# Building the one-hot products of a PEER layer in batches of eight tokens, with the weight products on GpSimd

## The reference

```python
s1 = einsum('thd,hkd->thk', q[:, :, 0], sub_keys[:, 0])   # 8 heads, 128 keys
s2 = einsum('thd,hkd->thk', q[:, :, 1], sub_keys[:, 1])
v1, i1 = top_k(s1, 16);  v2, i2 = top_k(s2, 16)
sc, ci = top_k(all sums v1 + v2, 16)
e = i1[ci // 16] * 128 + i2[ci % 16]                       # 8 * 16 = 128 experts per token
g = softmax(sc)
out[t] = sum over the 128 (e, g) of token t:  gelu(x_t . u_tab[e]) * g * v_tab[e]
```

## Time and profile before

| | |
|---|---|
| device time, three runs | 1741.38, 1743.40, 1743.91 us (median 1743.4) |
| span of the profiled execution | 1738.7 us |
| between span and the three runs | 2.7 to 5.2 us |
| stage that builds G, first to last DVE instruction | 536.9 to 657.8 us |
| DVE busy over the span | 1554.8 us (89%) |
| POOL busy over the span | 654.3 us (38%) |

### The profile page before, as it was taken

How to read it: one execution, slowest core, us unless ns; L and a number is a source line. 1 busy time by engine, 2 the same in 40 slices (tenths; PEclk the granted TensorE clock), 3 DMA queues, 4 the chain that set the end, 5 groups by cost and what they waited for, 6 DMA issues and landing times.

```text
span 1738.7 us, 29907 instructions
## 1 busy us (share of the span) xinstructions
PE 1666.5 (96%) x9344; PEld 1402.2 (81%) x9344; DVE 1554.8 (89%) x3196; ACT 866.7 (50%) x2431; POOL 654.3 (38%) x644
## 2 busy tenths in 40 slices
PE   6999999999966999999999999999999999999997
PEld 4566777866645788899989999999999988999996
DVE  3887863499999999999999999999999999999998
ACT  3222564346778995444444444444444444444443
POOL 0000000034557994444444444344444444443442
PEclk9999999999977999999999999999999999999999
DMA  9343202211135779999999999999999999999996
GB/s 357 125 141 123 74 1 78 71 61 49 61 121 173 223 201 346 396 389 401 408 395 401 405 407 401 403 409 395 396 407 399 396 406 400 402 402 403 400 400 211
DMA packets 129316, 505.91 MB, mean 291 GB/s; under 512 B 9184, under 2 KB 64096, under 8 KB 79968
## 3 DMA queue, kind: packets, MB, share of 16 engines
q0 software_dynamic: 36864, 268.45, 38.3%
q1 hardware_dynamic: 92096, 236.49, 36.5%
q10 hardware_dynamic: 288, 0.13, 0.0%
HBM read 477.18 MB, written 25.10 MB: 289 GB/s over the span
## 4 chain that ended last, share of the span: by engine, by line
DVE 35%; DMA 23%; PE 19%; issue 19%; ACT 2%; POOL 2%; DVEq 1%; SPq 0%; POOLq 0%; ACTq 0%
DMA slab<-table,ixr 22%; DVE slab L1745 9%; PE psum L501 7%; DVE slab L1695 5%; DVE ulo L1636 4%; PE psum L736 3%; DVE slab L1735 3%; DVE slab L1699 2%; DVE vlo L1722 2%; DVE slab L1730 2%; PE psum L502 2%; PE psum L666 1%; DVE wlo L1718 1%; POOL slab L1876 1%; DVE slab L1550 1%
## 5 line engine op out<-in xcount | busy, mean ns | idle before, releaser
L1876 POOL DMA_INDIRECT slab<-table,ixr x256 | 421.5, 1647 | 603.8 <-DVE slab L1745 552.2
L848 PE MATMUL psum<-hhi,uhi 128*128 128x384 f32 x1008 | 338.8, 336 | 2.4 <-issue 2.1
L848 PE MATMUL psum<-hhi,ulo 128*128 128x384 f32 x1008 | 338.2, 335 | 0.0
L848 PE MATMUL psum<-hlo,uhi 128*128 128x384 f32 x1008 | 337.6, 335 | 0.0
L1745 DVE SCALAR_TENSOR_TENSOR slab<-slab,cf 128x1024 f32<-128x1024 f32 x252 | 323.3, 1283 | 14.8 <-DVE slab L1745 0.5
L1735 DVE SCALAR_TENSOR_TENSOR slab<-slab,h2tok 128x1024 f32<-128x1024 f32 x256 | 312.2, 1220 | 26.5 <-DMA slab<-table,ixr 26.2
L862 PE MATMUL psum<-vhi,whi 128*128 128x512 f32 x762 | 297.1, 390 | 3.1 <-DVE wlo L1718 3.1
L862 PE MATMUL psum<-vhi,wlo 128*128 128x512 f32 x762 | 299.7, 393 | 0.0
L862 PE MATMUL psum<-vlo,whi 128*128 128x512 f32 x762 | 299.2, 393 | 0.0
L501 PE MATMUL psum<-slab 128*128 128x512 f32 x464 | 239.1, 597 | 2.1 <-ACT slab L929 1.7
L1210 ACT CAST whi<-slab 128x384 fp32r<-128x384 f32 x127 | 65.3, 514 | 306.7 <-DVE slab L1730 306.7
(11 more groups left out here) (237 smaller groups left out, 2801.3 us busy)
## 6 DMA issues: line engine op xcount, KB each, us to landing
slab<-ublk SPq DMA_DIRECT2D x64, 1024.0 KB
slab<-vtab SPq DMA_DIRECT2D x63, 1024.0 KB
slab<-wblk SPq DMA_DIRECT2D x90, 512.0 KB, 4.6
g_dram<-slab SPq DMA_DIRECT2D x11, 1984.0 KB, 9.0
slab<-g_dram SPq DMA_DIRECT2D x31, 704.0 KB, 8.9
slab<-table,ixr POOLq DMA_INDIRECT x256, 9.2
slab<-slab SPq DMA_DIRECT2D x42, 64.0 KB, 10.1
x<-x_in SPq DMA_DIRECT2D x1, 2560.0 KB, 9.6
```

What stands on the lines that cost most here:

```text
L848: last = pe.matmul(psum[:, b, 0:ND], w[:, c, :], m[:, c, :], start=(m_ == 0), stop=(m_ == 3 * DC - 1))
L1876: pool.indirect_dma_start(out=rows[:, sl % GR, :], out_offset=None, in_=table, in_offset=bass.IndirectOffsetOnAxis(ap=ixr[:, half, half_co ...
```

## The change

G is built in 48 batches of 8 tokens instead of 96 steps of 4. For each batch:

- DVE compares a constant `iota8` (bf16, each key number eight times) with `e2b` (bf16, the second halves) in one `tensor_tensor` of 1024 elements per partition, and writes the bf16 result to `same` (two buffers).
- DVE makes all eight `hot_a` rows in one float32 `tensor_tensor` of 1024 elements.
- POOL multiplies `same` with `gT` in one `tensor_tensor` of 1024 elements, which writes all eight `hot_b` rows (two buffers of eight rows). In batches 2 and 3 (`FETCH_IN`) DVE makes four of the rows and POOL four, and POOL issues two row fetches after each.
- ACT makes no rows. It copies PSUM out as before, in steps of 4 tokens, and no longer prepares the negated weights.
- PE issues the same matmuls in the same order; it waits for the makers at every second step.

`iota8` is filled once by a DVE `tensor_copy` before the search.

```diff
-FETCH_AT = (2, 3, 4, 5)
+BATCH = 8
+NB = ND // BATCH
+FETCH_IN = (2, 3)
...
+        iota8 = sb("iota8", [P, KEYS, BATCH], BF16)
+        e2b = sb("e2b", [P, ND], BF16)
+        e1T, gT = (sb(n, [P, ND]) for n in ("e1T", "gT"))
...
+        def by_vector(n):
+            return BATCH // 2 if n in FETCH_IN else 0
...
             for b in range(ND // 4):
+                at, half = divmod(b, 2)
+                if not half:
+                    pe.wait_ge(hot_a_set, at + 1)
+                    pe.wait_ge(hot_b_set, at + 1)
+                    if at in FETCH_IN:
+                        pe.wait_ge(hot_d_set, FETCH_IN.index(at) + 1)
                 if b >= 4:
                     pe.wait_ge(g_laid, b - 3)
                 for m in range(4):
+                    last = pe.matmul(psum[:, 4 + b % 4, m * P:(m + 1) * P], hot_a[:, at % 2, 4 * half + m, :], hot_b[:, at % 2, 4 * half + m, :], start=True, stop=True)
...
-            def distance(b):
-            def hot_row(b):
...
+            step(v.tensor_copy(iota8[:], con[:, C_IOTA:C_IOTA + KEYS].unsqueeze(2).broadcast_to([P, KEYS, BATCH])))
             v.tensor_copy(count, con[:, C_AT:C_AT + CAND].unsqueeze(2).broadcast_to([P, CAND, EARLY])).then_inc(topk_step, 1)
...
+            def hot_batch(n):
+                col, b = first_token(n), n % 2
+                if n >= 2:
+                    v.wait_ge(hot_b_set, n - 1)
+                if n - 2 in FETCH_IN:
+                    v.wait_ge(hot_d_set, FETCH_IN.index(n - 2) + 1)
+                v.tensor_tensor(same[b], iota8[:], e2b[:, col:col + BATCH].unsqueeze(1).broadcast_to([P, KEYS, BATCH]), ALU.is_equal).then_inc(same_set, 1)
+                if n >= 2:
+                    v.wait_ge(g_made, 2 * n - 2)
+                wide = [P, BATCH, KEYS]
+                v.tensor_tensor(hot_a[:, b], con[:, C_IOTA:C_IOTA + KEYS].unsqueeze(1).broadcast_to(wide),
+                                e1T[:, col:col + BATCH].unsqueeze(2).broadcast_to(wide), ALU.is_equal).then_inc(hot_a_set, 1)
+                m = by_vector(n)
+                if m:
+                    v.wait_ge(same_set, n + 1)
+                    v.tensor_tensor(hot_b[:, b, 0:m].rearrange("p t k -> p k t"), same[b][:, :, 0:m],
+                                    gT[:, col:col + m].unsqueeze(1).broadcast_to([P, KEYS, m]), ALU.mult).then_inc(hot_d_set, 1)
...
+            for n in range(NB):
+                col, b, m = first_token(n), n % 2, by_vector(n)
+                if n % (P // BATCH) == 0:
+                    pool.wait_ge(slot_set, n * BATCH // P + 1)
+                if n >= 2:
+                    pool.wait_ge(g_made, 2 * n - 2)
+                pool.wait_ge(same_set, n + 1)
+                pool.tensor_tensor(hot_b[:, b, m:BATCH].rearrange("p t k -> p k t"), same[b][:, :, m:BATCH],
+                                   gT[:, col + m:col + BATCH].unsqueeze(1).broadcast_to([P, KEYS, BATCH - m]), ALU.mult).then_inc(hot_b_set, 1)
+                if n == FETCH_IN[0]:
+                    pool.wait_ge(row_numbers_set, 1)
+                    pool.tensor_copy(ixr[:, 0, :], idxf[:, 0:8]).then_inc(ix_copied, 1)
+                    pool.wait_ge(ix_copied, 1)
+                if n in FETCH_IN:
+                    for sl in (2 * FETCH_IN.index(n), 2 * FETCH_IN.index(n) + 1):
+                        fetch_row(sl, 0, sl)
```

More of the change, by code:

```diff
@@ L263, in build @@
         e1u, e2u = (view(n, P).bitcast(U32) for n in (0, P))
-        gnT, away = view(38016, ND), view(256, 4, KEYS)
+        same = [view(c0, KEYS * BATCH // 2).bitcast(BF16).rearrange("p (k t) -> p k t", t=BATCH) for c0 in (256, 37248)]
         v_raw0 = view(35584, D)
-        hot_a, hot_b = view(9216, 4, 4, P), view(3072, 4, 4, P)
+        hot_a, hot_b = view(9216, 2, BATCH, P), view(3072, 2, BATCH, P)
         gbuf = view(19456, 2, KEYS, TG)
@@ L820, in _ @@
             for b in range(ND // 4):
-                pe.wait_ge(hot_a_set, sum(hot_a_split(n) > 0 for n in range(b + 1)))
-                pe.wait_ge(hot_b_set, b + 1)
-                pe.wait_ge(hot_c_set, b + 1)
+                at, half = divmod(b, 2)
[4 more added lines that the diff above has]
+                        pe.wait_ge(hot_d_set, FETCH_IN.index(at) + 1)
                 if b >= 4:
                     pe.wait_ge(g_laid, b - 3)
+                elif b + 4 in SLOT_BANK:
+                    pe.wait_ge(slot_set, SLOT_BANK.index(b + 4) + 1)
                 for m in range(4):
-                    last = pe.matmul(psum[:, 4 + b % 4, m * P:(m + 1) * P], hot_a[:, b % 4, m, :], hot_b[:, b % 4, m, :], start=True, stop=True)
+                    last = pe.matmul(psum[:, 4 + b % 4, m * P:(m + 1) * P], hot_a[:, at % 2, 4 * half + m, :], hot_b[:, at % 2, 4 * half + m, :], start=True, stop=True)
                 last.then_inc(g_made, 1)
@@ L1667, in number_halves @@
                 step(v.tensor_copy(e1T[:, part], e1u[:]))
-                step(v.tensor_copy(e2T[:, part], e2u[:]))
+                step(v.tensor_copy(e2b[:, part], e2u[:]))
             def halves_ready():
@@ L1688, in _ @@
             for k in range(N_DENSE):
                 v.wait_ge(slot_set, k + 1)
-                for b in range(k * P // 4, (k + 1) * P // 4):
-                    if b >= 4:
-                        v.wait_ge(g_made, b - 3)
-                    for m in range(3):
-                        col = token_of(b) + m
-                        v.tensor_scalar(hot_b[:, b % 4, m, :], con[:, C_IOTA:C_IOTA + KEYS], e2T[:, col:col + 1], gT[:, col:col + 1],
-                                        ALU.is_equal, ALU.mult)
-                    m0 = hot_a_split(b)
-                    col, wide = token_of(b) + m0, [P, 4 - m0, KEYS]
-                    v.tensor_tensor(hot_a[:, b % 4, m0:4, :], con[:, C_IOTA:C_IOTA + KEYS].unsqueeze(1).broadcast_to(wide),
-                                    e1T[:, col:col + 4 - m0].unsqueeze(2).broadcast_to(wide), ALU.is_equal).then_inc(hot_b_set, 1)
-                    within = b % (P // 4)
+                for n in range(k * P // BATCH, (k + 1) * P // BATCH):
+                    hot_batch(n)
+                    within = n % (P // BATCH)
@@ L1702, in _ @@
                     if k + 1 < N_DENSE:
[L1703 removed]
+                        if within == 9:
                             split_number(k + 1)
[L1705 removed]
+                        elif within == 10:
                             number_halves(k + 1)
[L1707 removed]
+                        elif within == 11:
                             halves_ready()
[L1709 removed]
+                    if n == 0:
@@ L1710, in _ @@
                         late_sums()
-                    elif k == 0 and within == 1:
                         row_numbers()
```

53 lines of the change are left out of this document (4 added, 49 removed).

## The result

The changed kernel takes 1801.34 us (median of 4 runs, 1797.90 to 1803.44), the kernel before 1742.39 us (median of 4). The ratio is 1.0339, with a 95% interval from 1.0322 to 1.0356: 59 us slower. The profiled execution of the changed kernel took 1802.85 us with a span of 1801.0 us.

What follows compares the result with a forecast made beforehand. DVE was taken to bound the kernel, with only the stage building G affected: 51.6 us more there, plus 0.6 and 0.5, lose 52.7 us; 1743.4 + 52.7 = 1796.1 us, range 1772 to 1822 us for 8 in 10.

Steps and rivals of the forecast that it cites:

- Exclusion of VectorE and GpSimd: Stage building G: while one engine streams two tensors, the other's waits, both ways; handover 0.01 to 0.05 us; forecast chance 0.77.
- The rival without sharing: Stage building G: path not shared in this way; 2.1 then 2.35 us a batch, 1734.9 us in all; chance 0.07.
- the one in which the bf16 comparison is exempt: Stage building G: only float32 instructions exclude POOL; period 2.95 us, 1770 us in all; chance 0.11, including sharing in parts.
- The period: Per batch of the stage: streaming 0.55 + 1.05 + 1.77 = 3.37 us, handovers and starts about 0.13 us, together 3.5 us.
- the bound from two float32 inputs: POOL's product: upper bound of 2.2 us streaming, from 2.12 ns an element; 1813 to 1818 us; chance 0.2 within the forecast.
- The estimate from the Trainium skill, GPSIMD Engine Reference, section 3.1: POOL's product: 2.25 us for 1024 elements, from 4497 ns for 2048; by it period 3.9 us, time 1815 us.
- The stage: Building G: 48 x 3.5 + 3 (other DVE work) + 1.5 = 172.5 us, 51.6 more than 120.9.
- The fetches in batches 2 and 3: POOL's row fetches, in pairs behind half a product: 8.8 us against 7.0 in the period; taken as +1.5 us.
- The 0.6 us for `iota8` and 0.5 us for the end: Filling iota8 on the chain, +0.6 us; PE's two steps left behind the last product, +0.5 us.
- The rival, over 5 us lost by the clock: Stage building G: TensorE's clock falls to its lower level, costing over 5 us on top; chance 0.05.
- `hot_a` stays at 1.20 us while products run beside it: Profile of the stage after the change: a sign that would show the prediction wrong.
- The main loop unchanged within 1 us: Profile after the change: main loop expected to stay within 1 us, as the change adds and removes nothing there.

Runs made afterwards that it cites:

- the layout run: hot_b laid out key by key, so GpSimd's product reads and writes contiguously and TensorE reads with a stride, against the changed kernel: 1813.11 us.
- the one with mixed engines: Against the changed kernel, per batch: three hot_a rows on GpSimd by tensor_scalar, five products on VectorE, three on ScalarE, hot_b layout kept: 1834.83 us.

## Why the prediction was right, and where it was off

The forecast was 1796 us in a range of 1772 to 1822; 1801.3 us were measured, 59 us more than before against 52.7.

- **Exclusion of VectorE and GpSimd.** Right for VectorE's two-tensor instructions and GpSimd's product, and shown from both sides: a two-tensor instruction added to VectorE costs its full 1.14 us a batch, a MAX8 of the same length nothing, and with GpSimd's product taken away the kernel gets faster. The rival without sharing (1734.9 us, period under 2.45) and the one in which the bf16 comparison is exempt (period 2.95) are out: `same` waits for the product in 38 of 48 batches, 2.63 us for 0.68, and in the others it was not issued beside one.
- **The period.** 3.5 us were forecast and 3.68 measured. The mis-sized term is the product's streaming time: 1.77 us taken, 2.01 measured. The rows I took it from the earlier trace rows have the types but another broadcast; the bound from two float32 inputs, 2.17 us, was also off. The strided write is not the cause, as the layout run shows. Alone the product takes 2.15 us, where I had 1.95. The estimate from the Trainium skill, GPSIMD Engine Reference, section 3.1, was 2.25 us for the whole instruction: nearer to the 2.15 us than mine, and as far off as mine if it is taken as streaming time. (Put into the sum for 1.77 us as it stands, 2.25 us gives a period of 3.98 us and 1819 us, not the 3.9 us and 1815 us that I wrote.) The other terms made up for 0.05 us of the 0.24: `same` 0.54 us (0.55 forecast), and 1.13 us for `hot_a` with its handover, where I had 1.05 us and 0.13 us for all handovers. Part of the closeness of the forecast is therefore luck: errors that offset each other.
- **The stage.** From the first `same` at 535.3 us to the end of the last product at 716.2 us: 180.9 us against 172.5 forecast. The period makes 48 x 0.18 = 8.6 us of it; the rest cancels, the fetches being dearer and the other VectorE work cheaper than forecast. The fetches in batches 2 and 3 were put at +1.5 us; from `hot_a` of batch 2 (543.50) to that of batch 6 (560.58) it is 17.1 us, 2.4 more than four periods, with `hot_a` of batch 5 caught behind two products and 3.16 us of waiting for PE ahead of it. With 48 x 3.68 = 176.6 us for the periods and 2.4 us here, 1.9 us are left for the other VectorE work, for which I had 3 us. That work, "one input", I took as free of the exclusion; its casts and `tensor_scalar` are not, though that cost little: the four distances from batch to batch with one of them held up are 3.96 us in place of 3.69.
- **The 0.6 us for `iota8` and 0.5 us for the end.** Both right within 0.1 us: `iota8` took 0.68 us, and from the end of the last GpSimd product to the first dot product (719.71) there are 3.5 us, against 3.1 before from the last `hot_a`. The stage nevertheless began 1.6 us earlier than before (535.3 for 536.9 us). Its start moves by as much between kernels that are alike up to there (first `hot_a` at 535.8, 537.5 and 540.4 us in three of the experiments), and I have not looked for the cause.
- **TensorE's clock.** The granted clock was 1.00 from 580 us on, with the weight loads busy 11.33 of 20 us in the stretch shown, and did not fall again in the stage. It rose later than before: 0.67 in the mean from 540 to 560 us, where it had been 0.88. The rival, over 5 us lost by the clock, did not come true. That was not sure: in the run with a second two-tensor instruction and in the one with mixed engines the clock did fall within the stage.
- **The signs of being wrong.** "`hot_a` stays at 1.20 us while products run beside it" came out word for word: the product is recorded from 579.80 us on, inside `hot_a`, which keeps its 1.21 us. The sign was badly chosen, as the one issued second waits, and that is the product; it is `same` and the product that show the exclusion. "The main loop unchanged within 1 us" was not met either in the profiled executions (3.6 us longer); between the experiments it moves by 5.1 us, so that limit was too tight for single executions.
- **What the profile of before had hidden.** I wrote that sharing hardly mattered before because POOL's instructions have one tensor. That reason was wrong. One-tensor rows do wait for VectorE's two-tensor instructions. It mattered little since those were short, one in a step: L1910 took 677 ns in the mean, against 0.60 us with VectorE waiting, so by estimate under 0.1 us a row, on an engine that was not on the chain.

The engine counts explain why the idea looked good: VectorE's own work per 8 tokens fell from 2.45 to 1.75 us, ScalarE lost its 1.8 us of row making (four instructions of 0.41 and 0.49 us), and PE had the room. But GpSimd's 2 us came on top of VectorE's and not beside it. None of the versions tried is faster than the kernel before; the best, with ScalarE in GpSimd's place, is 0.8% slower, since there a `hot_b` row costs VectorE 0.30 us (0.90 us for four products, and an eighth of the 0.60 us for `same`), a little more than the direct comparison with multiplication before (0.26 us from start to start, 0.336 as recorded), and GpSimd's `hot_a` rows are missing.

## What to carry to other kernels

Where GpSimd runs `tensor_tensor` or copies, add up their streaming time and that of VectorE's two-tensor instructions as if the two were one engine; work that moves from the one to the other while both are in use is not taken off the path. GpSimd's `tensor_scalar` is another case: it waits for VectorE's two-tensor instructions but hardly holds them up. In a profile the sign is an instruction that lasts longer than its shortest record and ends its own streaming time behind the end of the other engine's. On VectorE, MAX8 and reductions ran beside GpSimd's product unhindered, casts and `tensor_scalar` did not, though they read one tensor too. ScalarE's rows took 0.42 us each beside a VectorE that was busy all the time; whether GpSimd holds ScalarE up was not tested by itself.

## What the runs showed of the hardware that was not expected

- GpSimd's tensor_scalar with 1024 elements, bf16 to float32, took 3.7 us in the median, its two-tensor product of the same size 2.15 us alone. Three of 128 elements took 1.76 us alone, 0.60 each.
- VectorE's bf16 by float32 product takes 0.68 us for 512 elements when both sides are contiguous and 1.04 to 1.06 us when the write or the bf16 read has a stride (512 bytes between elements of the write, 16 bytes of the read). GpSimd shows no such difference for the write (2.00 and 2.01 us of streaming), and 0.2 us for the read at 1024 elements (2.21 us).
- A stride of 32 bytes in the float32 moving operand of a 128x128x128 matmul raises its records from 275 to 412 ns, and 16 of them from 2.02 to 3.75 us.
